# Modulation tiles ahead of waiting weight halves, the gate's low rank between query and key panels, and the last feed-forward block's hidden tile in the input memory, in a four-layer fp32 network

## The reference, cut to what matters

```python
mods = jnp.split(c_act @ w_ada[i] + b_ada[i], 6, axis=-1)      # (1024) @ (1024, 6144)
u = x * (1.0 + sc1) + sh1
proj = u @ w_in                                # q 512, k 512, v 1024, g 1024, gk_lr 16 columns
log_a = log_sigmoid(gk_lr @ w_gk2 + b_gk) / 16
cum = cumsum(log_a within a chunk of 64)       # per head of 128 key features, 4 heads
a_fwd = (q * exp(cum)) @ (k * exp(-cum)).T ; a_bwd = (q * exp(-cum)) @ (k * exp(cum)).T
o = where(lower, a_fwd, a_bwd) @ v + (q * exp(cum)) @ state     # state: 128 x 256 per head
state = state * exp(cum_end) + (k * exp(cum_end - cum)).T @ v
y = (rms_normed(o) * g_norm * silu(g)) @ w_out
# feed-forward, after layer norm and modulation:
y = square(relu(u @ w1)) @ w2                  # 1024 -> 4096 -> 1024
```

## Time and profile before

| | us |
|---|---|
| median of 3 runs | 2028.55 (2026.88 to 2029.15) |
| the profiled execution, its own time | 2032.37 |
| its span in the trace | 2030.6 |
| TensorE matmul busy | 1848.4 (91%) |
| VectorE busy | 1185.5 (58%) |
| ScalarE busy | 753.7 (37%) |
| GpSimd busy | 802.3 (40%) |
| granted TensorE clock, mean | 0.950 |

### The profile page before, as it was taken

How to read it: one execution, slowest core, us unless ns; L and a number is a source line. 1 busy time by engine, 2 the same in 40 slices (tenths; PEclk the granted TensorE clock), 3 DMA queues, 4 the chain that set the end, 5 groups by cost and what they waited for, 6 DMA issues and landing times.

```text
span 2030.6 us, 25040 instructions
## 1 busy us (share of the span) xinstructions
PE 1848.4 (91%) x9107; PEld 1486.9 (73%) x9107; DVE 1185.5 (58%) x1780; ACT 753.7 (37%) x1181; POOL 802.3 (40%) x577
## 2 busy tenths in 40 slices
PE   4985789999999899989999999997999899989989
PEld 3763567778888777777877888886788777667767
DVE  5683234877777671555378677777298733116562
ACT  3232244422222243555153222233435544445451
POOL 4430223466556525322255555653323343432222
PEclk7987899999999899989999999998999999989999
DMA  8652112565554413221255555541122122222111
GB/s 316 207 172 72 58 61 74 188 207 160 174 166 150 155 54 112 83 73 53 63 176 168 180 175 161 164 155 55 53 80 68 63 64 83 84 83 73 64 52 42
DMA packets 116902, 235.68 MB, mean 116 GB/s; under 512 B 8112, under 2 KB 25392, under 8 KB 115792
## 3 DMA queue, kind: packets, MB, share of 16 engines
q1 hardware_dynamic: 113776, 227.17, 34.0%
q10 hardware_dynamic: 3040, 7.34, 1.1%
HBM read 232.36 MB, written 2.13 MB: 115 GB/s over the span
## 4 chain that ended last, share of the span: by engine, by line
PE 38%; issue 35%; POOL 19%; DVE 6%; ACT 2%; POOLq 0%; DVEq 0%; ACTq 0%
PE bank L216 18%; POOL wsp L2133 18%; PE bank L416 8%; PE bank L1219 2%; PE bank L1260 2%; PE bank L1223 1%; PE bank L1330 1%; PE bank L1314 1%; PE bank L1291 1%; PE bank L1718 1%; PE bank L1495 1%; ACT wsp L179 1%; PE bank L304 0%; DVE fP L1392 0%; DVE hst L1951 0%
## 5 line engine op out<-in xcount | busy, mean ns | idle before, releaser
L2133 POOL TENSOR_TENSOR wsp<-raw,wsp 128x512 fp32r<-128x512 f32 x528 | 789.2, 1526 | 1208.4 <-ACT wsp L179 1208.4
L216 PE MATMUL bank<-xT,wsp 128*128 128x512 f32 x2592 | 610.3, 395 | 9.9 <-POOL wsp L2133 6.1
L216 PEld LDWEIGHTS bank<-xT,wsp 128*128 128x128 f32 x2592 | 489.8, 190 | 122.7 <-issue 9.6
L179 ACT ACTIVATE wsp<-raw 128x2048 fp32r<-128x2048 f32 x132 | 252.0, 1913 | 638.1 <-PE bank L216 275.3
L416 PE MATMUL bank<-wsp,hT 128*128 128x512 f32 x1536 | 369.6, 401 | 19.0 <-DVE hT L518 10.4
L416 PEld LDWEIGHTS bank<-wsp,hT 128*128 128x128 f32 x1536 | 294.3, 192 | 91.6 <-DVE hT L518 10.6
L216 PE MATMUL bank<-wsp,xT 128*128 128x512 f32 x1248 | 310.2, 405 | 25.3 <-DVE gg L1095 20.3
L216 PEld LDWEIGHTS bank<-wsp,xT 128*128 128x128 f32 x1248 | 238.1, 194 | 85.8 <-DVE gg L1095 22.5
L530 DVE TENSOR_TENSOR htmp<-bank,gate 128x512 f32<-128x512 f32 x112 | 76.9, 687 | 57.9 <-PE bank L416 57.9
L518 DVE TENSOR_TENSOR hT<-h,hT 128x512 fp32r<-128x512 f32 x64 | 95.3, 1548 | 15.5 <-ACT hT L479 15.5
L513 DVE TENSOR_TENSOR h<-h 128x512 f32<-128x512 f32 x64 | 56.9, 904 | 80.6 <-ACT h L474 80.3
(11 more groups left out here) (301 smaller groups left out, 2045.6 us busy)
## 6 DMA issues: line engine op xcount, KB each, us to landing
raw<-in_ff_w SPq DMA_DIRECT2D x64, 1024.0 KB, 5.5
ada_ring<-in_w_ada SPq DMA_DIRECT2D x48, 384.0 KB, 3.9
ada_ring<-in_ada_w SPq DMA_DIRECT2D x48, 384.0 KB, 3.6
ring<-in_w_ada SPq DMA_DIRECT2D x64, 256.0 KB, 4.8
raw<-in_odd_w_in SPq DMA_DIRECT2D x16, 1024.0 KB, 5.5
raw<-in_gla_w_in SPq DMA_DIRECT2D x12, 1024.0 KB, 5.6
raw<-in_att_w_in SPq DMA_DIRECT2D x12, 1024.0 KB, 5.2
raw<-in_even_w_in SPq DMA_DIRECT2D x12, 1024.0 KB, 5.1
```

Source lines behind the costliest of these rows:

```text
L179: act.activation(wsp[:, slot, 0], raw[:, slot], ACT.Copy).then_inc(hi_made, 1)
L216: mm = pe.matmul(out_ap, l, r, start=(start and n == 0), stop=(stop and n == 2))
L2133: ins = pool.tensor_tensor(wsp[:, slot, 1, k], raw[:, slot, k], wsp[:, slot, 0, k].bitcast(F32), ALU.subtract)
```

## The change

**Tile order.** SP sends 8 tiles behind each of halves 2 to 7, 7 behind each of halves 8 and 9, and none behind 10 and 11. VectorE takes 20 tiles, the gates and `to_end` of heads 0 and 1, then 14 tiles, then 2 at each of 15 steps.

```diff
-                for g in range(g, g + (8 if j < 6 else 5)):
-                    ada0_tile(g)
-                g += 1
+                n = 8 if j < 8 else 7 if j < 10 else 0
+                for k in range(g, g + n):
+                    ada0_tile(k)
+                g += n
...
-            modulation(range(0, 34))
-            n = 34
+            modulation(range(0, 20))
+            for h in range(2):
+                gates(h)
+                to_end(h)
+            modulation(range(20, 34))
             for i in range(4 * 8):
-                if i < 20:
-                    modulation(range(n, n + 2 - i % 2))
-                    n += 2 - i % 2
+                if i < 15:
+                    modulation(range(34 + 2 * i, 36 + 2 * i))
```

```diff
             low_rank()
+            for h in range(2):
+                for t in range(ST):
+                    pe_piece(pe, "gla_in", "in_gla_in", 1, 4, "T", h, t, free, ST)
+                if h == 0:
+                    gate_logits(0)
+                    gate_logits(1)
             for i in range(4 * 8):
                 piece(i)
-                if i == 1:
-                    gate_logits()
-                for h, at in enumerate((4, 6, 15, 18)):
+                if i == 0:
+                    gate_logits(2)
+                    gate_logits(3)
+                for h, at in enumerate((1, 3, 13, 15)):
                     if i == at:
                         turned(h)
-                for h, at in enumerate((5, 7, 16, 19)):
+                for h, at in enumerate((2, 4, 14, 18)):
                     if i == at:
                         scores(h)
-                for h, at in enumerate((10, 13, 24, 27)):
+                for h, at in enumerate((8, 11, 24, 27)):
                     if i in (at, at + 1):
                         chunk_states(h, i - at)
-                for h, at in enumerate((12, 17, 26, 30)):
+                for h, at in enumerate((10, 17, 26, 30)):
                     if i == at:
                         output(h)
...
+            act_ahead(act, "gla_in", 0, 0)
+            for t in range(ST):
+                query_key(0, t)
+            act.wait_ge(gkT_done, 1)
+            act.activation(gkT[:, :], bank[GLA_S][:, :], ACT.Copy).then_inc(s["gkT"], 1)
+            act_ahead(act, "gla_in", 1, 0)
+            softplus(0)
+            softplus(1)
+            for t in range(ST):
+                query_key(1, t)
+            exps(0)
+            exps(1)
```

**Last feed-forward block.** Block 7's hidden tile goes to `xT`, and its `high` and `low` stand before the casts and the adds:

```diff
                 act_high(act, q, 1)
+                if last:
+                    high(m, xT)
                 act_high(act, q + 1, 0)
                 act_high(act, q + 1, 1)
-                high(m)
-            with act.Fori(1, FB) as m:
+                if not last:
+                    high(m, hT[l])
+            with act.Fori(1, FB - 1) as m:
                 step(m)
+            step(FB - 1, True)
...
                 ada(i + 1, range(0, 4))
                 square(i + 1)
+                if last:
+                    low(i + 1, xT)
                 ada(i + 1, range(4, 6))
                 add(i, 0, peel)
                 ada(i + 1, range(6, 8))
                 add(i, 1, peel)
-                low(i + 1)
+                if not last:
+                    low(i + 1, hT[l])
```

More of the change, by code:

```diff
@@ L415, in down_tile @@
                     for q, (a, c) in enumerate(PASSES):
-                        mm = pe.matmul(bank[bk][:, :], hT[l][:, a, k, t * P:t * P + P], wsp[:, n, c, k, :],
+                        mm = pe.matmul(bank[bk][:, :], h[:, a, k, t * P:t * P + P], wsp[:, n, c, k, :],
                                        start=(k == 0 and q == 0), stop=(k == HK - 1 and q == 2))
@@ L485, in act_ff, with step @@
             act_high(act, b // 2 + 1, 1)
-            high(0)
-            def step(m):
+            high(0, hT[l])
+            def step(m, last=False):
                 q = b // 2 + 2 * m
@@ L558, in ada, with step @@
                                  16 * (KT // RING * m + k // RING + 1), s["ada_used"], KT * m + k)
-            def step(i, peel=False):
+            def step(i, peel=False, last=False):
                 ada(i + 1, range(0, 4))
                 square(i + 1)
+                if last:
+                    low(i + 1, xT)
                 ada(i + 1, range(4, 6))
@@ L572, in dve_ff @@
             square(0)
-            low(0)
+            low(0, hT[l])
             step(0, True)
-            with dve.Fori(1, FB - 1) as i:
+            with dve.Fori(1, FB - 2) as i:
                 step(i)
+            step(FB - 2, last=True)
             before_last()
@@ L839, in gla_o, with gla_pre @@
             return bank[(GLA_KV if h == GLA_H - 1 else GLA_O) + c // 2][:, (c % 2) * GLA_DV:(c % 2) * GLA_DV + GLA_DV]
+        def gla_pre(h):
+            return bank[h if h < 2 else 4 + h][:, :]
         def gla_pe(pe):
@@ L865, in low_rank @@
                 pe.wait_ge(lohi_made, 2)
-                pe.wait_ge(free, KT + ST)
+                pe.wait_ge(free, KT + 1)
                 for k in range(KT):
@@ L871, in low_rank, with gate_logits @@
                 mm.then_inc(gkT_done, 1)
-            def gate_logits():
-                pe.wait_ge(gk2_ld, 16)
-                pe.wait_ge(s["gkT"], 1)
-                pe.wait_ge(free, KT + 2 * ST)
-                for h in range(GLA_H):
-                    pe.matmul(bank[4 + h][:, :], wgk2[:, h * P:h * P + P], gkT[0:GLA_R, :], start=True, stop=True)\
-                      .then_inc(s["pre"], 1)
+            def gate_logits(h):
+                if h == 0:
+                    pe.wait_ge(gk2_ld, 16)
+                    pe.wait_ge(s["gkT"], 1)
+                pe.wait_ge(free, KT + ST if h < 2 else KT + 2 * ST)
+                pe.matmul(gla_pre(h), wgk2[:, h * P:h * P + P], gkT[0:GLA_R, :], start=True, stop=True).then_inc(s["pre"], 1)
             def turned(h):
@@ L958, in gla_act, with query_key @@
             free = TS["in_gla_in"]["bank_free"]
-            act.wait_ge(gkT_done, 1)
-            act.activation(gkT[:, :], bank[GLA_S][:, :], ACT.Copy).then_inc(s["gkT"], 1)
+            def query_key(seq, t):
+                if t == 3:
+                    act_ahead(act, "gla_in", seq, 1)
+                wait_tile(act, "gla_in", seq, t)
+                act.activation((gq, gk)[seq][:, t], bank[4 * seq + t][:, :], ACT.Copy).then_inc(free, 1)
             def evac(i):
@@ L980, in softplus @@
                     act.wait_ge(s["a"], h - 1)
-                achain(act, act.activation(t, bank[4 + h][:, :], ACT.Abs, bias=col("gla_b_gk", h)))
+                achain(act, act.activation(t, gla_pre(h), ACT.Abs, bias=col("gla_b_gk", h)))
                 achain(act, act.activation(t, t, ACT.Exp, scale=-1.0))
@@ L1002, in squares @@
                 act_inverse_root(act, grs[:, h], gss[:, h], sd[:, :], 1.0 / GLA_DV, RMS_EPS).then_inc(s["ss"], 1)
+            act_ahead(act, "gla_in", 0, 0)
[6 more added lines that the diff above has]
+            softplus(1)
+            for t in range(ST):
+                query_key(1, t)
+            exps(0)
+            exps(1)
             for i in range(4 * 8):
-                for h, at in enumerate((1, 1, 6, 8)):
+                for h, at in enumerate((None, None, 3, 5)):
                     if i == at:
                         softplus(h)
-                for h, at in enumerate((2, 3, 13, 16)):
+                for h, at in enumerate((None, None, 11, 14)):
                     if i == at:
                         exps(h)
-                for h, at in enumerate((4, 6, 15, 18)):
+                for h, at in enumerate((1, 3, 13, 15)):
                     if i == at:
                         keys(h)
-                for h, at in enumerate((13, 18, 27, 31)):
+                for h, at in enumerate((11, 18, 27, 31)):
                     if i == at:
@@ L1034, in gates @@
                     dve.wait_ge(s["exps"], 3 * h - 3)
-                dchain(dve, dve.tensor_scalar(c, bank[4 + h][:, :], col("gla_b_gk", h), 0.0, ALU.add, ALU.min))
+                dchain(dve, dve.tensor_scalar(c, gla_pre(h), col("gla_b_gk", h), 0.0, ALU.add, ALU.min))
                 dve.tensor_tensor(c, c, gkf[:, h % 2], ALU.subtract).then_inc(s["la"], 1)
@@ L1054, in scaled @@
                 dve.wait_ge(s["exps"], 3 * h + 3)
+                if h == 1:
+                    dve.wait_ge(s["pre"], GLA_H)
                 dve.scalar_tensor_tensor(gqb[:, r], q, sc, gkf[:, r], ALU.mult, ALU.mult).then_inc(s["qk"], 1)
@@ L2153, in _ @@
             act_transposed(act, "in_gla_in", scale_at, bias_at)
-            def fn(b, t, ps):
-                return act.activation((gq, gk)[b][:, t], ps[:, :], ACT.Copy)
-            act_evac(act, "gla_in", "in_gla_in", 0, fn)
-            act.preload_act_table_set(LN_EXP)
             gla_act(act)
```

28 lines of the change are left out of this document (15 added, 13 removed).

## The result

The change takes 2003.25 us (median of 4 runs, 2002.59 to 2004.76) against 2028.85 us in runs on the same chip (2026.88 to 2032.29): a ratio of 0.9873, 95% interval 0.9856 to 0.989. The forecast was 1992, with a range of 1979 to 2010. The direction and the range hold; of the 36 us forecast, 25.6 came, and 2003.25 lies outside the forecast's own range of 1985 to 2001. The profiled executions are 29.8 us apart (2032.37 and 2002.59, spans 2030.6 and 2000.9), because that of before was slower than each of its timed runs.

What follows compares the result with a forecast made beforehand. TensorE bounds the kernel, with time won only where it idles or runs at the lower clock. Stage 28 plus feed-forwards 8 gives 36 us: 1996 profiled, 1992 median; own range 1985 to 2001, wider range 1979 to 2010.

Steps and rivals of the forecast that it cites:

- the first rival: The start eats more: piece 5 ends 6 us later, another 4 to 6 us wait, stage gives 14, about 2008; chance 0.18.
- the stage: Panel 0 through attention piece 24: piece 24 ends near 223 with clock loss instead of 251.4, winning 28 us, bounds 15 to 38.
- The feed-forward part: Last hidden block of both feed-forwards, low parts moved ahead: 4.8 and 3.6 us won, 8 together, bounds 5 and 13.
- the wait of 4 to 5 us before the second chunk-state part: TensorE ready 12.6 us after piece 5, VectorE's states at 17: a wait of 4.5 us.
- The ring: TensorE waits for VectorE, VectorE for a tile, tile behind a half, half for TensorE; idles of 14.87 and 14.05 us.
- The walk up to piece 5: Start of the stage: half 5 issued at 97.6, ke at 116.2, piece 5 ends near 136 with three fewer pieces done.
- the gate products: VectorE's gate products 0 and 1 stand behind the states of head 1: waits of 2.7 and 2.3 us.
- The first turn's wait: TensorE at the turn of head 0, behind VectorE's tiles and scaling: a wait of 3.7 us.
- the queue is then nearly empty, so I take 5.5: Landing time of half 5 after its issue: 5.5 us, from rows of 4.9 to 7.7, median 5.3.
- From piece 5 to piece 24: Work of 72.5 us and waits of 10.5, piece 24 ending at 219; 4 us for the clock added after.
- The start alone loses some 3 to 5 us: Up to piece 5: its end near 136, against near 140 before with three more pieces done.
- I count 0.6 of its 2.5 as won: First feed-forward's last block still starts at the slow clock, 24.98 against 22.47 us; 0.6 us counted as won.

Runs made afterwards that it cites:

- the kernel without the gate move: Tile order and feed-forward part put onto the kernel before, gate logits and gates left in their old places: 1984.02 us, ratio 0.9772.
- half 5 earlier: Whole change, but SyncE sends weight half 5 behind tile 21 instead of tile 25: 2004.67 us, ratio 0.9867 to the kernel before.
- fewer tiles first: Whole change, but VectorE takes 26 modulation tiles ahead of its first scaling instead of 36: 2010.77 us, ratio 0.9902 to the kernel before.
- both: Whole change with half 5 sent behind tile 21 and 26 tiles ahead of the first scaling: 2004.85 us, ratio 0.9875 to the kernel before.

## Why the prediction was right or wrong, by its steps

The forecast was 1992 and 2003.25 came, nearer to the first rival (2008). The mechanism of both gains was right. The forecast promised too much because it priced the gate move too low: the stage won 16.9 us, not 28. The feed-forward part gave 4 us more than forecast and hid some of that. Of the signs it named, four held: the tile waits (18.6 us, none over 10), the wait of 4 to 5 us before the second chunk-state part, the gate logits' wait for ScalarE, and last blocks without a gap. Four did not: an idle over 7 us came (8.68), the first turn was at 120.53 and not soon after 116, piece 24 ended at 234.50 and not by 230, and the first feed-forward's last block ran at a clock of 1.00, not 0.50.

**The ring and the tile order: right.** No wait of VectorE for a tile is over 4.5 us, and both long TensorE waits went. That the tile order breaks the ring is shown: it was run alone. Its worth was hidden in the forecast's sum; alone it is 33.9 us.

**The walk up to piece 5.** The wait at the second chunk-state part (4.5 forecast, 4.36 measured) is as worked out, and the gate products too (2.7 and 2.3; 2.92 and 2.45). The first turn's wait agrees by luck (3.7 forecast, 3.72 measured). Both engines were some 4 us later than forecast, and 3.7 isn't what the forecast's own times give: gate logits at 106.0, 2.4 for them and a piece of 2.8 end at 111.2, 5.0 ahead of its 116.2. Gate logits 2 and 3 wait 8.68, not 5.0: half 5 went out at 98.83, not 97.6, and landed in 7.3 us, not 5.5 ("the queue is then nearly empty, so I take 5.5"), and TensorE was ready 1.1 us sooner. ScalarE's timeline shows the cast beginning at once at the landing:

```profile
106.12 1.91 ACT L179 ACTIVATE wsp<-raw 128x2048 fp32r<-128x2048 f32 x1 [11.03 <-DMA raw<-in_gla_w_in]
107.94 0.58 ACT L983 ACTIVATE gk<-bank 128x512 f32<-128x512 f32 x1
```

The issue was late since the gates of head 0 took longer beside GpSimd's split of half 4. From VectorE's timeline, head 0, then head 1:

```profile
88.88 1.70 DVE L1071 TENSOR_TENSOR gcum<-gcum,gkf 128x512 f32<-128x512 f32 x1
90.62 2.20 DVE L1073 TENSOR_TENSOR_SCAN gcum<-u,gcum 128x512 f32<-128x512 f32 x1
...
94.24 0.69 DVE L1071 TENSOR_TENSOR gcum<-gcum,gkf 128x512 f32<-128x512 f32 x1
94.96 1.22 DVE L1073 TENSOR_TENSOR_SCAN gcum<-u,gcum 128x512 f32<-128x512 f32 x1
```

and, on GpSimd:

```profile
86.23 5.50 POOL L2173 TENSOR_TENSOR wsp<-raw,wsp 128x512 fp32r<-128x512 f32 x4 [5.54 <-ACT wsp L179]
```

That is 2.0 us which the forecast's 3.4 per head left out. The turn of head 1 waited 0.19, not 2.5. Piece 5 ends near 138.9 (pieces 5 to 8 begin at 136.08), against 136: 2.9 missed, as the first turn came 4.3 late and 1.4 of that was won back.

**From piece 5 to piece 24.** 95.6 us instead of the 87 forecast (72.5 of work, 10.5 of waits, 4 of clock). The waits are 16.0: two of 0.7 for a split that the forecast did not have, and 4.80 at the turn of head 3 instead of 1.0. There ScalarE casts half 8 from 189.63 to 191.5 ahead of the exponentials of head 3, and VectorE scales in 1.46, 1.78 and 1.63 us where it takes 0.7 elsewhere. Of the other 3.1 us some 2 are the slower matmuls behind waits: 4.62, 4.61 and 4.42 us for twelve matmuls that take 2.8 to 3.0, and 2.07 for chunk states that take 1.13, together 6 where 4 were counted; the last 1 us was not traced. In sum 2.9 + 8.6 = 11.5 us, which is the stage's miss (234.5 against 223).

**The step that failed for the design.** "The start alone loses some 3 to 5 us" priced the gate move. For the start that was about right: when the scores of head 1 are done, at 136.08 with five pieces behind TensorE, the kernel without the gate move is at 140.52 with eight, so 4.4 us sooner but three pieces (8.4 us) short, 4.0 lost. What the move costs behind piece 5 the forecast did not set apart. Measured against the kernel without it, the gate move costs 17.1 us of the stage (234.50 against 217.40). At the second chunk-state part the whole change is 4.6 us behind (157.93 against 153.33) with two pieces fewer done (5.6 us), so 10.2 in all; the other 6.9 come later, 4.8 of them the turn of head 3. The forecast walked the new order and never the tile order by itself, so it could not see that one part paid for another. The first rival ("the start eats more": stage 14, 2008) named things that came: the turn near 120.7 and the slow landing of half 5. But they took 2.9 us at piece 5 where it had 6, and mending them (half 5 earlier, fewer tiles first, both) gave nothing. Moving the steps back gave 5.0 us, and VectorE's tile places then 6.6 to 8.1 more. That second figure is not a share of the 19 us by itself: with the steps moved back the change's rule puts 56 tiles ahead of the first states, in the whole change 52.

**The feed-forward part.** The 1.3 us lost in the block before came as 1.35 and 1.34, and the low parts took 6.47 us beside GpSimd (6.35 forecast). The term that was mis-sized is the clock: "I count 0.6 of its 2.5 as won". In the first feed-forward the whole 2.9 us came back (24.98 to 22.07), in the second 0.7 (24.36 to 23.66), and the one-column matmuls ahead of it went from 4.24 to 3.63. In all 12.2 us came in place of 8. The Trainium skill (TensorE: Matmul & The Clock Gate, HAM oscillation — how this bites in real kernels) says that idle gaps between matmuls throttle the array; the forecast set it aside, and by it this part would have been 12. The first feed-forward of this trace bears it out, the second only in part, and that the sum came near 12 is partly luck: in other traces the first block too fell without a gap (last section).

**What stays open.** Whether a gate move could pay at all: with steps and tiles of before and half 5 earlier it is level with the version without it (0.9786 against 0.9772, overlapping intervals), so no gain of it is shown. Counted from the start of panel 0, its stage is 2.1 us shorter (170.7 against 172.8), less than the times can tell apart. The gate move with SyncE's tile order of before wasn't tried, nor were VectorE's tile places of before with the change's steps, so how the 19 us split between steps and tile places is open. The fastest version measured is tile order and feed-forward part alone.

## What to carry to other kernels

Moving a step earlier on one engine pays only if what releases it moves too: here the attention steps hung on VectorE's stream of tiles, and each piece that TensorE no longer had ahead of them was lost time. When a table of places is shifted, count for each step the work ahead of it on the waiting and on the releasing engine. A wait taken away at one place can come back whole at the next, as it did in four of the versions above, so the end of the stage is what counts. And price each part of a change by itself, since a large gain hides a loss: the sum was within its range while one of three parts cost 19 us.

## What the runs showed of the hardware

The granted clock can fall with TensorE busy throughout, and need not. In the version with fewer tiles first, the same one-column matmuls and last block as in the whole change, without a gap between them, took 4.07 and 24.82 us against 3.63 and 22.07. From the table by windows, us, PE, PEld, DVE, ACT and POOL busy, granted clock, DMA share and GB/s:

```profile
660.00:685.00 25.00, 23.92 (x104) 19.05 (x103) 20.96 (x21) 6.39 (x7) 12.78 (x8) 1.00 0.45 154
685.00:714.00 29.00, 29.00 (x131) 24.39 (x130) 23.30 (x38) 8.48 (x14) 5.42 (x4) 0.88 0.15 50
```

and the like stretch of the whole change:

```profile
684.00:706.00 22.00, 22.00 (x97) 18.01 (x96) 19.55 (x34) 6.78 (x13) 3.89 (x3) 1.00 0.15 48
```

In the first feed-forward the last block took 22.05 to 22.07 us in eight of the twelve traces with this part, 23.65 in one and 24.55 to 24.82 in three; the program there is the same in all. In the second feed-forward none of the twelve had 22.07; its block took 23.65 to 24.86 us. There the whole change's clock fell inside the block with TensorE busy throughout:

```profile
1348.00:1352.00 4.00, 4.00 (x12) 3.11 (x12) 3.57 (x5) 0.00 (x0) 2.75 (x3) 0.60 0.02 1
1352.00:1370.00 18.00, 18.00 (x81) 14.91 (x80) 16.59 (x25) 3.41 (x9) 0.00 (x0) 1.00 0.18 58
```

What decides it no run here shows; a forecast should carry these 2.8 us as a range, where this one took a single row for a rule.

VectorE's tensor_tensor on two inputs took 1.70 us beside GpSimd's split and 0.69 alone, the scan 2.20 and 1.22. The Trainium skill (GPSIMD Engine Reference, Specifications) says that GpSimd shares its memory interfaces with VectorE, with contention for VectorE instructions that have two inputs there; the rows agree.
